# Two transformer blocks in one kernel: the delta rule's first round begins inside the input products, and the modulation vector comes from raw weights

## What is computed

```
z = rmsnorm(x) @ w_in
qkv, gate, a_logit, b_logit, cfm_in = split(z)
qkv = silu(causal_dwconv(qkv, taps=4));  q, k = l2norm(q), l2norm(k)
g = -exp(a_log) * softplus(a_logit + dt_bias);  beta = sigmoid(b_logit)
o = gated_delta_rule(q, k, v, g, beta)
o = rmsnorm(o) * silu(gate)
c = silu(layernorm(causal_dwconv(glu(cfm_in), taps=31) + bias))
y = concat(o, c) @ w_out
mod = silu(c_2) @ w_ada + b_ada          (second block: a vector of 3072)
```

## Time and profile before

| | |
|---|---|
| median of three runs | 3157.41 us (3155.44 to 3160.51) |
| profiled execution, its own time | 3157.72 us |
| its span, first to last instruction | 3155.9 us |
| mean granted TensorE clock | 0.959 |
| TensorE (PE) busy | 2884.7 us (91%) |
| VectorE (DVE) busy | 1688.0 us (53%) |
| POOL busy | 1085.6 us (34%) |
| ScalarE (ACT) busy | 688.0 us (22%) |

### The profile page before, as it was taken

How to read it: one execution, slowest core, us unless ns; L and a number is a source line. 1 busy time by engine, 2 the same in 40 slices (tenths; PEclk the granted TensorE clock), 3 DMA queues, 4 the chain that set the end, 5 groups by cost and what they waited for, 6 DMA issues and landing times.

```text
span 3155.9 us, 42491 instructions
## 1 busy us (share of the span) xinstructions
PE 2884.7 (91%) x18302; PEld 2592.3 (82%) x18302; DVE 1688.0 (53%) x2202; ACT 688.0 (22%) x1197; POOL 1085.6 (34%) x588
## 2 busy tenths in 40 slices
PE   6999777868998999999999987989999999899888
PEld 6887767768878988788888776779999999888888
DVE  3489678873412554544444486321565666355455
ACT  3011122213323410000000032111222222243321
POOL 6433141125532623323233335642232232212343
PEclk9999888888999999999999988999999999999998
DMA  5222322114321421111111134542333332446652
GB/s 195 69 80 93 96 81 72 47 44 157 112 66 69 157 83 54 54 40 54 40 40 54 54 127 147 167 140 81 101 108 101 118 107 78 149 152 212 229 207 94
DMA packets 148067, 325.62 MB, mean 103 GB/s; under 512 B 11148, under 2 KB 77608, under 8 KB 147752
## 3 DMA queue, kind: packets, MB, share of 16 engines
q10 hardware_dynamic: 105832, 169.80, 15.8%
q1 hardware_dynamic: 42048, 153.11, 15.1%
HBM read 245.26 MB, written 77.61 MB: 102 GB/s over the span
## 4 chain that ended last, share of the span: by engine, by line
PE 75%; DVE 13%; ACT 4%; issue 2%; POOL 2%; ACTq 2%; DMA 2%; DVEq 0%; POOLq 0%
PE pp L232 27%; PE pp L217 21%; PE pp L416 8%; PE pp L1702 5%; PE pp L2219 4%; POOL w_lo L2776 1%; PE pp L1612 1%; DVE ffn_cb L1875 1%; PE pp L1592 1%; PE pp L369 1%; DVE hgin_b L2048 1%; POOL w_hi L2774 1%; PE pp L1261 1%; PE pp L2453 1%; PE pp L2452 0%
## 5 line engine op out<-in xcount | busy, mean ns | idle before, releaser
L2774 POOL CAST w_hi<-w_raw 128x1024 fp32r<-128x1024 f32 x292 | 349.2, 1196 | 2021.3 <-PE pp L232 917.4
L232 PE MATMUL pp<-w_hi,act_hi 128*128 128x256 f32 x2688 | 778.9, 290 | 52.1 <-ACT hg_st L2088 23.2
L232 PE MATMUL pp<-w_lo,act_hi 128*128 128x256 f32 x2688 | 766.5, 285 | 0.0
L232 PE MATMUL pp<-w_hi,act_lo 128*128 128x256 f32 x2688 | 766.3, 285 | 0.0
L2776 POOL TENSOR_TENSOR w_lo<-w_raw,w_hi 128x1024 fp32r<-128x1024 f32 x292 | 744.4, 2549 | 23.4
L232 PEld LDWEIGHTS pp<-w_hi,act_hi 128*128 128x128 f32 x2688 | 522.3, 194 | 60.0 <-issue 24.5
L232 PEld LDWEIGHTS pp<-w_lo,act_hi 128*128 128x128 f32 x2688 | 522.1, 194 | 0.0
L232 PEld LDWEIGHTS pp<-w_hi,act_lo 128*128 128x128 f32 x2688 | 521.3, 194 | 0.0
L217 PE MATMUL pp<-act_hi,w_hi 128*128 128x512 f32 (+1 forms) x976 | 300.7, 389 | 1.6 <-POOL w_lo L2776 1.6
L217 PE MATMUL pp<-act_lo,w_hi 128*128 128x512 f32 (+1 forms) x976 | 300.5, 389 | 0.0
L217 PE MATMUL pp<-act_hi,w_lo 128*128 128x512 f32 (+1 forms) x976 | 300.4, 389 | 0.0
(11 more groups left out here) (398 smaller groups left out, 4311.9 us busy)
## 6 DMA issues: line engine op xcount, KB each, us to landing
w_raw<-in_weights SPq DMA_DIRECT2D x292, 512.0 KB, 3.8
z_s<-hg_st ACTq DMA_DIRECT2D x24, 1024.0 KB, 4.5
hg_qkb<-hT_s ACTq DMA_DIRECT2D x24, 512.0 KB, 6.2
qkvT_s<-mixin_o ACTq DMA_DIRECT2D x12, 512.0 KB, 2.9
gdn_qkv<-qkvT_s ACTq DMA_DIRECT2D x8, 768.0 KB, 6.4
front_x<-in_x ACTq DMA_DIRECT2D x8, 512.0 KB, 7.4
mix_x<-in_x ACTq DMA_DIRECT2D x8, 512.0 KB, 6.2
x_s<-mix_y ACTq DMA_DIRECT2D x8, 512.0 KB, 3.1
```

The lines of the kernel that those rows point to most:

```text
L232: last = pe.matmul(dst, a[:, k, t * P:(t + 1) * P], w[slot][:, k * SC:k * SC + n], start=(k == 0 and a is high and w is w_hi), stop=(k == ...
L2774: pool.tensor_copy(hi, raw).then_inc(w_split, 1)
```

## The change

It does the following.

- The ab strip comes before qkv in the stream, and its product, transposes and copies before the qkv jobs or beside the first two.
- MixIn has no barrier at its end and no gate jobs. The gate is made in 16 units (gate_unit) in TensorE's queue of round -1: units 0 to 3 at the start, 4 behind the norm sums, 5 behind the decay sums, 6 and 7 to 8 behind the kk and kq products, 9 to 15 behind the last transposes (ct) of the preparation. ScalarE evicts and stores them two units at a time (keep_gate), 0 and 1 early in the round, 2 to 7 behind the decay exponentials. TensorE begins round 0 when the last is evicted.
- The delta rule's parameter loads, its first exponentials and first small VectorE steps move between the qkv jobs; the first qkv tile is loaded when all qkv stores have landed, the sums follow in round -1. ScalarE loads a table there for silu and one for exp.
- Of the 124 long taps 93 are done within the jobs (3 instead of 2 before the first short tap, no tail), 23 in round -1 and 8 in round 0.
- The modulation strips are no longer split. Each is 8 fp32 matmuls from w_raw with the fp32 vector ada_c; TensorE itself releases the halves of w_raw (w_ready). POOL skips these strips. There are two strips in round -1, two in round 0, the second at the round's end, and one in rounds 1 to 8 (ADA).
- Buffers are placed anew so that nothing of the delta rule's first round lies on what MixIn still reads.

The core of the diff:

```diff
-ORDER = [("k", N_K), ("v", N_V), ("cfm", N_CFM), ("qkv", N_QKV), ("ab", N_AB), ("gate", N_GATE), ("ada", N_ADA),
+ORDER = [("k", N_K), ("v", N_V), ("cfm", N_CFM), ("ab", N_AB), ("qkv", N_QKV), ("gate", N_GATE), ("ada", N_ADA),
...
+            def gate_unit(self, pe, u):
+                h, j = u // 2, FIRST_STRIP["gate"] + u // NT
+                if u % NT == 0:
+                    weights_ready(pe, j)
+                if u % 2 == 0:
+                    if h < 2:
+                        after(pe, self.shorts, f"tap9.{GTAPS - 1}", 0)
+                    elif h == 4:
+                        pe.wait_ge(self.delta.prep_dve, 10)
+                    else:
+                        after(pe, self.an, f"gate{(0, 0, 0, 1, 0, 2, 3, 4)[h]}", 0)
+                last = product_rows(pe, j % 2, u % NT, bank(self.GATE_BANKS[h])[:, u % 2 * SC:(u % 2 + 1) * SC], frees=(u % NT == 0))
+                if u % 2:
+                    last.then_inc(self.made, 1)
+            def keep_gate(self, act, h):
+                s, strip, pair = h % 2, h // 4, h % 4
+                act.wait_ge(self.made, self.AB + 2 + 12 + h + 1)
+                if h >= 2:
+                    act.wait_ge(self.gate_stored[s], 16 * (h // 2))
+                self.an.done(act.activation(self.gst[s][:, :, :], bank(self.GATE_BANKS[h]).rearrange("p (t n) -> p t n", t=2), ACT.Silu), f"gate{h}")
+                after(act, self.an, f"gate{h}", 0)
+                act.dma_start(gate_s.rearrange("(t p) n -> p t n", p=P)[:, 2 * pair:2 * pair + 2, strip * SC:(strip + 1) * SC],
+                              self.gst[s][:, :, :]).then_inc(self.gate_stored[s], 16)
...
+                        self.delta.load_params(act)
+                    if r == 8:
+                        self.delta.first_exps(act)
...
-                for s in range(2):
-                    act.wait_ge(self.stored[s], 16 * 6)
-                    act.wait_ge(self.gate_stored[s], 32)
+                self.qkv_stored(act)
...
+                    if r < 2:
                         after(pe, self.glus, f"glu{(job - 3) // 2}", 0)
+                    elif r == 2:
+                        after(pe, A, "ab1", 0)
                     else:
-                        after(pe, self.shorts, f"tap{job - 3 - 2 * CT}.{GTAPS - 1}", 0)
+                        after(pe, self.shorts, f"tap{r - 3}.{GTAPS - 1}", 0)
                     weights_ready(pe, j)
                     done(product_T(pe, j % 2, r % 2, self.dst(job), frees=(r % 2 == 0)))
+                    if r == 0:
...
-                    long(14 if c < 3 else 2)
-                dve.wait_ge(self.ada, 18)
-                dve.tensor_tensor(ada_l[:, :], self.cc[:, :], ada_h[:, :].bitcast(F32), ALU.subtract)
+                    long(14 if c < 3 else 3)
                 for r in range(12):
                     short(r)
                     long(4)
-                long(CT * CTAPS)
+                    if r == 5:
+                        self.delta.first_steps(dve)
+                    if r == 9:
+                        self.delta.second_steps(dve)
+                self.long = long
...
-            ADA = (3, 1, 1, 1, 1, 1, 1, 1, 1, 1, 0)
+            ADA = (2, 2, 1, 1, 1, 1, 1, 1, 1, 1, 0)
...
+                load(0)
+                after(act, self.src.an, f"src{CT - 1}", 0)
+                load(1)
+                load_bias(0)
...
                         prior(act, self.is_, "d6", p - 2)
                         P_.done(act.activation(self.Tm[p % 2][:, :, :], self.unit(), ACT.Copy), "ti")
+                    if p == 0:
+                        self.src.keep_gate(act, 0)
+                        self.src.keep_gate(act, 1)
+                        sums()
                     if inv:
...
                         P_.done(act.activation(self.xm[:, :, :], self.xm[:, :, :], ACT.Exp, scale=-1.0), "dec")
                         P_.done(act.activation(self.x[:, :, :], self.x[:, :, :], ACT.Exp), "decT")
+                    if p == 0:
+                        for h in range(2, self.src.GATES):
+                            self.src.keep_gate(act, h)
+                        act.preload_act_table_set("natural_log_exp_and_others")
+                        self.src.gates_stored(act)
+                        load_gate(0)
+                        load_gate(1)
                     if inv:
                         self.copy_y(act, i, 4)
...
+                def sums():
+                    pe.wait_ge(self.prep_dve, 8)
+                    after(pe, self.src.shorts, f"tap11.{GTAPS - 1}", 0)
+                    g = self.by_pair(self.g[:, :, :])
+                    for a, part in enumerate((upto, self.down)):
+                        pe.matmul(bank(self.O1)[:, a * 16:a * 16 + 16].rearrange("p (t h) -> p t h", t=NT), part[:, :], g[:, :, a, :], start=True, stop=True)
+                    pe.matmul(bank(self.O1)[:, 32:64], ones[:, :], self.g[:, :, :].rearrange("p t h -> p (t h)"), start=True, stop=True).then_inc(self.prep_pe, 1)
                 def ada(j, k0, k1):
                     strip = FIRST_STRIP["ada"] + j
-                    slot = strip % 2
                     if k0 == 0:
-                        weights_ready(pe, strip)
                         if j:
                             pe.wait_ge(self.ada_kept, j)
+                        else:
+                            weights_ready(pe, strip - 1)
                         if prep:
                             after(pe, self.pv, "l3", p)
                     for k in range(k0, k1):
-                        for a, w in ((ada_h, w_hi), (ada_h, w_lo), (ada_l, w_hi)):
-                            last = pe.matmul(bank(self.K_)[0:1, 0:SC], a[:, k:k + 1], w[slot][:, k * SC:(k + 1) * SC],
-                                             start=(k == 0 and a is ada_h and w is w_hi), stop=(k == NK - 1 and a is ada_l))
-                            if k == 0 and a is ada_h and w is w_hi:
-                                last.then_inc(w_used, 1)
+                        if k % (NK // 2) == 0:
+                            pe.wait_ge(w_loaded[k // (NK // 2)], (strip + 1) * 16)
+                        last = pe.matmul(bank(self.K_)[0:1, 0:SC], ada_c[:, k:k + 1], w_raw[:, k * SC:(k + 1) * SC], start=(k == 0), stop=(k == NK - 1))
+                        if k == 0:
+                            last.then_inc(w_used, 1)
+                        elif k == NK // 2 - 1:
+                            last.then_inc(w_ready, 1)
                     if k1 == NK:
-                        last.then_inc(self.ada_made, 1)
+                        last.then_inc(w_ready, 1)
                 def y(i, l):
...
+                    gates(0, 1, 2, 3)
+                    if p == 0:
+                        sums()
+                    if r == 0:
+                        after(pe, self.src.an, f"gate{self.src.GATES - 1}", 0)
...
                         PP.done(last, "ss")
+                        gates(4)
...
                         PP.done(last, "gb")
+                        gates(5)
...
                         PP.done(last, "kk")
+                        gates(6)
...
                         PP.done(last, "kq")
+                        gates(7, 8)
-                    for j in jobs[:1]:
+                    for j in jobs[:1] if r >= 0 else ():
-                    for j in jobs[:1]:
+                    for j in jobs[:1] if r >= 0 else ():
+                    if r == 0:
+                        after(pe, self.src.longs, f"tap{CT - 1}.{CTAPS - 1}", 0)
...
                         PP.done(last, "ct")
+                        gates(*range(9, 16))
-                    for j in jobs[1:]:
+                    for j in jobs[1:] if r >= 0 else jobs:
...
-                prep_step(dve.memset(self.S[:, :, :], 0.0))
+                def long(*counts):
+                    if -1 <= r < len(counts) - 1:
+                        self.src.long(counts[r + 1])
...
+                        long(9)
+                        if p == 0:
+                            self.src.qkv_stored(dve)
+                        if p == 0:
+                            sums()
+                        if p == 1:
+                            self.src.gates_stored(dve)
+                            self.prep_step(dve, dve.memset(self.S[:, :, :], 0.0))
+                    long(1, 2)
                     if inv:
...
+                        if p == 0:
+                            dve.wait_ge(self.prep_act, 7)
+                    long(0, 2)
                     if inv:
...
+                    long(1, 2)
                     if inv:
...
+                    long(0, CT * CTAPS)
                     if inv:
...
+                    long(2, 0)
                     if state:
...
-                    for j in self.ada_of(r)[:1]:
+                    for j in self.ada_of(r)[:1] if r >= 0 else ():
-                    for j in self.ada_of(r)[1:]:
+                    long(10)
+                    for j in self.ada_of(r)[1:] if r >= 0 else self.ada_of(r):
...
             for j in range(NSTRIPS):
```

(10 more changed lines are left out.)

234 lines of the change are left out of this document (117 added, 117 removed).

## The result

The changed kernel ran in 3138.69 us (median of 5, 3134.92 to 3143.47), the kernel before in 3157.41 (3155.44 to 3163.27). The ratio is 0.9938, 95% interval 0.9921 to 0.9954: 18.7 us or 0.6% faster, where 29.0 had been forecast. The profiled execution is the slowest of the five, 3143.47 around a span of 3141.6, so the two traces differ by 14.3 only.

The account below looks back on a forecast made before the run. It took rounds 1 to 6 as bound by a ladder of steps between engines, neither full, delayed by POOL's split. -24.2 + 12.5 - 16 - 1.3 = -29.0 from 3157.7 gave 3128.7, stated as 3128.5; range 3112 to 3147.

Parts of the forecast that it names:

- Part 1: Up to round 0: gate units fill TensorE's waits and two raw modulation strips replace three; -24.2 us, ends -29 and -18.
- The rival of units at half clock: Gate units before round 0: waits drop TensorE's clock, each of 12 units costs 2.9 us more; +34.6, 3163 us, chance 0.06.
- Part 2: Round 0: gains eight long taps and a second strip, loses some stalls; +12.5 us, ends +8 and +17.
- the fallen clock that was allowed for: Start of round 1: a lower clock, allowed for in raising round 0's cost from 11.8 to +12.5 us.
- Part 3: Rounds 1 to 6: without POOL's split VectorE's stalls go, 2.4 to 2.8 us per round; -16, ends 0 and -24.
- The reason given for the part that doesn't come through: Rounds 1 to 6: TensorE's strip halves, 0.95 us longer each, are late next, so of 3.9 only 2.4 to 2.8 comes through.
- Part 4: Rounds 7, 8 and the first output strip: stalls lost, dearer strips paid, output split covered; -1.3 us, ends +3 and -3.
- the sum itself: Whole kernel: the four terms -24.2 + 12.5 - 16 - 1.3 = -29.0 us taken off the total time.
- the case of fillers that don't fill: Before round 0: gate weights, evictions or the tile load make units wait for each other; 10 us more, 3138.5, chance 0.10.

Follow-up runs that it names:

- e6: e5 with all 31 last long taps in the first preparation and none in round 0; 3110.7 us, ratio 0.9856 to the kernel before.
- e2: The kernel before with both halves of the modulation vector in one 64-byte slot, so every later tile moves down 64 bytes; 0.33% slower than the kernel before.
- e3: The kernel before with only the modulation from raw weights, no POOL split of these strips, addresses kept by a pad; 0.76% faster than the kernel before.
- e4: The changed kernel with POOL's split of the modulation strips put back, the reordering kept; 0.51% faster than the kernel before.
- e7: e5 with four of the eight products of each modulation strip left out in rounds 1 to 8, loads kept; 3113.5 us.
- e1: The changed kernel with an unused 64-byte pad behind the modulation vector, restoring the later tiles' addresses; 3128.83 us, ratio 0.9898 to the kernel before.
- e5: The changed kernel with the level stage's one-element tile placed ahead of its other tiles, moving those back 64 bytes; 3115.71 us, ratio 0.9869 to the kernel before.
- e9: The changed kernel run once more, unaltered; ratio 0.9952 to the kernel before.
- e10: The changed kernel with 128 unused bytes behind the modulation vector; ratio 0.9952 to the kernel before.
- e12: e6 with the modulation strip moved whole into TensorE's wait ahead of the kq products in even rounds alone; 3109.6 us.

## Why the prediction was right and where it was wrong

**Part 1, to the start of round 0: -24.2 forecast, -26.5 measured.** The gate units were fillers as computed: eleven at full clock took 31.7, the one ahead of them was at half clock, and VectorE was not the bound. The rival of units at half clock so came true for one unit of twelve. Two terms were off and partly cancelled. The tile landed 2.5 us earlier, its load having taken 5.02 us instead of 6.4 (the median of all eight such loads before; why this one was shorter is not shown), and the work behind it took 1.6 less, so the units ended at 381.4 and not 385.5. The two raw strips took 11.2 from there instead of 9.6: the load between them, 3.96, was exposed as computed, but the second strip ran partly at half clock, 5.29 for 3.8.

**Part 2, round 0: +12.5 forecast, +11.1 measured**, with the fallen clock that was allowed for (0.77; the first half of its strip took 2.49). e6 shows that the eight taps make up most of what it gained in length: without them 28.6.

**Part 3, rounds 1 to 6: -16 forecast.** 11.2 in five rounds is 2.24 each, a little below the 2.4 to 2.8; over all executions with split (before, e2) and whole strips it is 1.4 to 2.3. The mechanism is shown from both sides by e3 and e4: POOL's split stalls VectorE's operations with both inputs in SBUF, and without it the three take 0.47, 0.62 and 0.16 us. The reason given for the part that doesn't come through was TensorE's dearer strip. The chain has it there and VectorE now waits 1.04 for TensorE, but this step is neither shown nor refuted: in e7 half the strip is gone and the time is the same, but the granted clock is lower too (0.84 for 0.92).

**Part 4, the tail.** With round 6 it was -2.7 - 1.3 = -4.0; measured -4.3. That this agrees is luck: in e1, e5, e9 and e10, with the same code there, the stretch took 89.9 to 93.2 us at a clock of 0.83 to 0.88, so 7.3 to 10.6 less than before, and the profiled execution had 0.78. The first output strip was split by 684.1, 7.5 ahead of its product, as assumed.

Up to the output product this sums to -30.9 against -29.0. **The step that failed is the sum itself**: it ended with the modulation and took for granted that all behind it moves as a block. No part asked what the new layout does. The diff showed it (two tiles for one, ahead of the arena of every later stage), and the profile of before had a hint: L2776's mean over the kernel is 2549 ns where the pass that VectorE waited for took 2.37, so elsewhere POOL seems to have waited for VectorE, and there VectorE could come to wait for POOL. The terms left out are +18.6 for the level stage and some -3.5 for nine ffn cycles of 0.39; had they been in, the forecast would have stood at 3143.6. The second is smaller than what executions differ by: from the output product to the level stage it was 1361.0 us before, 1360.0 in the changed kernel and 1357.0 in e9. The measured 3138.69 lay within the range, and its distance from the forecast of 3128.5 comes from an effect that none of the rivals named: the case of fillers that don't fill gave the same time, 3138.5, and its mechanism did not occur. That the range held is luck in this respect.

## What to carry to other kernels

A change of the layout is a change of the whole kernel: after adding or dropping a tile, compare the stages that were not touched, by their own durations, before believing the total, and try a pad. Look for places where VectorE's operations with two inputs in SBUF meet POOL's splits: they cost each round of the delta rule some 2 us here, and in the level stage 64 bytes decided which of the two paid. And work taken from TensorE in a stop-and-go stretch was worth nothing in e7, with a lower granted clock: read the clock beside the time.

## What was not expected of the hardware

- Duration by address. With all tiles of a stage 64 bytes lower, a copy under a mask of 1024 elements took 1.32 us instead of 1.365, a product or difference of 512 elements 0.67 instead of 0.69, 60 products of TensorE 13.94 instead of 14.26. Why is open. In e10, 128 bytes above the changed kernel's place, the copy took 1.32 as well.
- Who wins. POOL's pass came 0.01 to 0.03 us behind VectorE's operation in both layouts. In one VectorE kept its turn over four operations, to 2393.59, and POOL took 4.74, to 2395.85, of which the last 2.26 are about the length of a pass alone; in the other POOL came in after the first. The Trainium skill (SBUF — State Buffer, section Who interferes with whom) says that the order of issue decides who blocks. The second case agrees; in the first, POOL's pass stands in the trace from 2391.11, VectorE's next operation only from 2391.69, and yet POOL waited for it and the two behind it. The measurement decides: in this kernel the order in which the two start in the trace does not tell alone. What about the addresses changes the turn is open.
- The clock as a hidden price: 0.92 with the whole strip, 0.84 with half of it, in five rounds of nearly the same length (164.0 and 164.7 us); and 0.95, then 0.80, from one stretch to the next in e12.
